# Down rows of the experts' MLP loaded as row pairs, 64 partitions and 8 KB each, with the inner columns transposed at a step of two

## The reference

```
DEPTH, SEQ, D_MODEL = 2, 256, 1024
N_EXPERTS, TOP_K_EXPERTS, D_FF_EXPERT = 8, 2, 2816

def swiglu(h, w_gate, w_up, w_down):
    a = jnp.einsum('bsd,df->bsf', h, w_gate)
    u = jnp.einsum('bsd,df->bsf', h, w_up)
    return jnp.einsum('bsf,fd->bsd', jax.nn.silu(a) * u, w_down)

def moe_swiglu(h, w_router, w_gate, w_up, w_down):
    logits = jnp.einsum('bsd,de->bse', h.astype(F32), w_router.astype(F32))
    top_val, top_idx = lax.top_k(logits, TOP_K_EXPERTS)
    top_w = jax.nn.softmax(top_val, axis=-1)
    combine = jnp.sum(jax.nn.one_hot(top_idx, N_EXPERTS, dtype=F32) * top_w[..., None], axis=-2)
    out = jnp.zeros_like(h)
    for e in range(N_EXPERTS):
        out = out + combine[..., e:e + 1].astype(h.dtype) * swiglu(h, w_gate[e], w_up[e], w_down[e])
    return out
```

## Time and profile before

| What | Value |
|---|---|
| runs | 1917.53, 1920.16, 1922.07 us; median 1920.16 us |
| profiled execution | 1927.55 us, of which the span of the records is 1925.7 us |
| mean granted TensorE clock | 0.98 |
| busy, share of the span | PE 95%, PEld 77%, DVE 74%, ACT 58%, POOL 20% |
| moved | 506.45 MB, mean 263 GB/s over the span |
| expert layer's loads | 176 transfers of 512 KB for each of gate, up and down |

### The profile page before, as it was taken

One profiled execution on the slowest core, in us unless ns is written; L12 is line 12 of the kernel. 1 busy time (PEld: TensorE's weight loads), 2 busy tenths in 40 slices (PEclk: granted clock), 3 DMA queues, 4 the chain that ended last, 5 costly groups with the idle time before them and its releaser, 6 DMA issues.

```text
span 1925.7 us, 26024 instructions
## 1 busy us (share of the span) xinstructions
PE 1832.6 (95%) x8799; PEld 1490.6 (77%) x8799; DVE 1420.1 (74%) x1631; ACT 1123.4 (58%) x1296; POOL 391.4 (20%) x315
## 2 busy tenths in 40 slices
PE   7899999989999997899989879999999999999997
PEld 5677886867888685788878667888888888888885
DVE  6647874465877477554566848898888888888897
ACT  5645443564444356344344727777777777777775
POOL 3722212453220365200036500000000000000000
PEclk9999999989999999899999989999999999999999
DMA  8338985416988441365645058999999999999994
GB/s 269 110 110 328 363 331 179 131 67 253 336 336 294 138 146 44 114 211 179 205 143 170 23 207 326 387 377 384 377 385 378 382 377 386 380 375 382 378 387 171
DMA packets 237934, 506.45 MB, mean 263 GB/s; under 512 B 23304, under 2 KB 74720, under 8 KB 231712
## 3 DMA queue, kind: packets, MB, share of 16 engines
q1 hardware_dynamic: 225664, 492.91, 70.5%
q0 software_dynamic: 3008, 10.32, 2.0%
q10 hardware_dynamic: 9184, 2.23, 0.5%
HBM read 497.49 MB, written 7.91 MB: 262 GB/s over the span
## 4 chain that ended last, share of the span: by engine, by line
PE 77%; DVE 8%; issue 7%; ACT 3%; POOL 2%; DMA 2%; SPq 0%; POOLq 0%; DVEq 0%; ACTq 0%
PE bank L2352 23%; PE bank L2354 23%; PE bank L2353 23%; PE bank L2471 2%; ACT slab L2043 1%; DVE slab L1291 1%; PE bank L2791 1%; POOL w_lo L827 1%; ACT w_hi L1893 1%; PE bank L2562 1%; PE bank L2540 1%; PE bank L2522 1%; DVE w_lo L978 1%; DMA slab<-in_w_mlp_out 1%; DMA slab<-in_w_router 1%
## 5 line engine op out<-in xcount | busy, mean ns | idle before, releaser
L978 DVE TENSOR_TENSOR w_lo<-slab,w_hi 128x2048 fp32r<-128x2048 f32 x369 | 847.3, 2305 | 219.0 <-ACT w_hi L1893 218.1
L1893 ACT ACTIVATE w_hi<-slab 128x2048 fp32r<-128x2048 f32 (+2 forms) x421 | 797.1, 1899 | 330.5 <-PE bank L2354 229.7
L2352 PE MATMUL bank<-w_hi,hT_hi 128*128 128x512 f32 (+3 forms) x1664 | 649.6, 390 | 15.0 <-DVE hT_lo L1027 4.3
L2354 PE MATMUL bank<-w_hi,hT_lo 128*128 128x512 f32 (+3 forms) x1664 | 638.1, 383 | 0.0
L2353 PE MATMUL bank<-w_lo,hT_hi 128*128 128x512 f32 (+3 forms) x1664 | 637.9, 383 | 0.0
L2352 PEld LDWEIGHTS bank<-w_hi,hT_hi 128*128 128x128 f32 x1664 | 316.4, 190 | 78.7 <-DVE w_lo L978 8.8
L2354 PEld LDWEIGHTS bank<-w_hi,hT_lo 128*128 128x128 f32 x1664 | 315.4, 190 | 59.7
L2353 PEld LDWEIGHTS bank<-w_lo,hT_hi 128*128 128x128 f32 x1664 | 316.4, 190 | 55.3
L827 POOL TENSOR_TENSOR w_lo<-slab,w_hi 128x512 fp32r<-128x512 f32 (+2 forms) x208 | 262.0, 1293 | 384.8 <-ACT w_hi L1893 365.2
L2352 PE MATMUL bank<-w_hi,hid_hi 128*128 128x512 f32 x680 | 266.6, 392 | 4.2 <-DVE hid_lo L1560 3.5
L2354 PE MATMUL bank<-w_hi,hid_lo 128*128 128x512 f32 x680 | 265.6, 391 | 0.0
(11 more groups left out here) (252 smaller groups left out, 1243.2 us busy)
## 6 DMA issues: line engine op xcount, KB each, us to landing
slab<-in_w_exp_gate SPq DMA_DIRECT2D x176, 512.0 KB, 7.0
slab<-in_w_exp_up SPq DMA_DIRECT2D x176, 512.0 KB, 7.2
slab<-in_w_exp_down SPq DMA_DIRECT2D x176, 512.0 KB, 6.9
slab<-in_w_ada SPq DMA_DIRECT2D x48, 1024.0 KB, 5.0
slab<-in_w_mlp_in SPq DMA_DIRECT2D x64, 512.0 KB, 6.2
slab<-in_w_mlp_out SPq DMA_DIRECT2D x64, 512.0 KB, 6.2
slab<-in_w_in SPq DMA_DIRECT2D x56, 512.0 KB, 5.0
slab<-in_w_out SPq DMA_DIRECT2D x32, 512.0 KB, 4.5
```

Of the source, the lines that this page charges most:

```text
L978: dve.tensor_tensor(w_lo[:, q, 0:n], raw(s)[:, 0:n], w_hi[:, q, 0:n].bitcast(F32), ALU.subtract).then_inc(lo_dve, 1)
L1893: act.activation(w_hi[:, q, 0:n], raw(s)[:, 0:n], ACT.Copy).then_inc(hi_done, 1)
L2352: pe.matmul(dst, a_hi, b_hi, start=start, stop=False)
L2354: return pe.matmul(dst, a_lo, b_hi, start=False, stop=stop_)
```

## The change

Three edits. The first is in how SP builds its transfers: `tile` makes the list of a tile's parts before it waits for the slot, where it made them one by one after the wait. The second is the layout of the experts' down tiles. `row_pairs` sees the weights as "(r p i) n -> p (a r) (i n)" with i = 2: partition p of row block r holds the rows 256 r + 2p and 256 r + 2p + 1, which lie side by side in memory, 8 KB. A tile is the same 256 rows and the same 1 MiB of memory as before, in another arrangement, and its two parts are partitions 64 to 127 and then 0 to 63, each 64 partitions x 8 KB. The third follows from the second: block i of a tile now holds every second down row, so `turn_hidden` with `pairs` set, which only the experts use, takes every second inner column of a block of 256 for each transpose. The other layers keep `rows` and plain columns.

```
--- before.py
+++ after.py
@@ -620,9 +620,10 @@
 
                 prev = ring.before_raw()
                 t, s, _, _ = ring.next()
+                moves = list(parts(raw(s)))
                 if prev is not None:
                     lo_wait(prev)
-                for dst, src in parts(raw(s)):
+                for dst, src in moves:
                     sp.dma_start(dst, src).then_inc(w_loaded[s], 16)
 
             def block_of(w, c, n, k0, nk):
@@ -654,6 +655,14 @@
                         d = r.rearrange("p (i n) -> p i n", i=2)
                         for i in (1, 0):
                             yield d[:, i:i + 1, :], w[:, bass.ds(r0 + 2 * b + i, 1), :]
+                    tile(parts)
+
+            def row_pairs(w, r0, n):
+
+                for b in range(n):
+                    def parts(r, b=b):
+                        for o in (P // 2, 0):
+                            yield r[o:o + P // 2, :].unsqueeze(1), w[o:o + P // 2, bass.ds(r0 + b, 1), :]
                     tile(parts)
 
             def ada_piece(l, k, n):
@@ -740,7 +749,8 @@
 
                         def weights(e):
                             return [A[n][0, bass.ds(e, 1)].rearrange("a (k p) n -> p (a k) n", p=P)
-                                    for n in ("w_exp_gate_2", "w_exp_up_2", "w_exp_down_2")]
+                                    for n in ("w_exp_gate_2", "w_exp_up_2")] + [
+                                        A["w_exp_down_2"][0, bass.ds(e, 1)].rearrange("a (r p i) n -> p (a r) (i n)", p=P, i=2)]
 
                         def body(i, p, n, first, last):
                             wg, wu, wd = weights(2 * i + p)
@@ -753,14 +763,14 @@
                                     sp.wait_ge(sc_done, 2 * (UNIT0[l] + UNITS[l]))
                                 cols(wg, wide_at(j + 1), F_WIDE)
                                 if narrow(j):
-                                    rows(wd, 0, 1)
+                                    row_pairs(wd, 0, 1)
                                 else:
-                                    rows(wd, 4 * j - 2, 2)
+                                    row_pairs(wd, 2 * j - 1, 2)
 
                             def final(j):
                                 if not last:
                                     gated(*weights(2 * i + p + 1)[:2], 0)
-                                rows(wd, 4 * j - 2, 2)
+                                row_pairs(wd, 2 * j - 1, 2)
 
                             step(0, first and n0 == 0)
                             step(1)
@@ -2464,12 +2474,16 @@
                         if c and not t:
                             between()
 
-            def turn_hidden(at, ntt, n, src, width_, dst):
+            def turn_hidden(at, ntt, n, src, width_, dst, pairs=False):
                 for t in range(ntt):
                     pe.wait_ge(sq_done, at + t + 1)
                     for f in range(n):
-                        ins = pe.transpose(dst[t][:, f * P:(f + 1) * P],
-                                           scr(src + t * width_ + f * P, P), ident)
+                        if pairs:
+                            two = scr(src + f // 2 * 2 * P, 2 * P).rearrange("p (q i) -> p i q", i=2)
+                            ins = pe.transpose(dst[t][:, f * P:(f + 1) * P], two[:, f % 2, :], ident)
+                        else:
+                            ins = pe.transpose(dst[t][:, f * P:(f + 1) * P],
+                                               scr(src + t * width_ + f * P, P), ident)
                     ins.then_inc(ht_done, 1)
 
             pe.wait_ge(c_in, 16)
@@ -2898,7 +2912,7 @@
                                 rows_of([bank[0]], listed_left, COL, 4, 4, False, True, 1)
 
                         def turn(j):
-                            turn_hidden(ub + n * MS + j, 1, 2 if narrow(j) else 4, X_MACT2, F_WIDE, [bank[0]])
+                            turn_hidden(ub + n * MS + j, 1, 2 if narrow(j) else 4, X_MACT2, F_WIDE, [bank[0]], True)
 
                         rows_up(0)
                         if not first:
```

4 lines of the change are left out of this document (2 added, 2 removed).

## The result

| What | Before | After |
|---|---|---|
| median of 4 runs | 1920.95 us (1917.53 to 1922.07) | 2261.24 us (2257.32 to 2266.44) |
| ratio to before, 95% interval | | 1.1768 (1.1743 to 1.1794) |
| span of the profiled execution | 1925.7 us | 2255.5 us |
| mean granted TensorE clock | 0.98 | 0.96 |

What follows compares the result with a forecast made beforehand. TensorE was taken to bound the kernel, with loads taking over after the change: +192.2 us for doubled down parts, -6.7 us at the tail, other terms nothing, +185.5 us in all, 2106 us; range 1917 to 2140 us.

Steps and rivals of the forecast that it cites:

- What bounds the kernel: Expert layer: TensorE sets the pace, 93.7 us per expert, waiting for no load; loads come early enough.
- 31 us of slack: Expert layer's loads: at 399 GB/s they would fit into 686 of 717.5 us, so slower loads use this up first.
- Two other signs: Expert layer, if right: down parts' time to landing grows above that of the others', and SP's waits stay.
- Half the partitions: Down tile loads: 64-partition parts cost between nothing and twice the time each; +192.2 us taken; chance of slowed loads 0.68.
- the slow end: Down parts: half the partitions find half of the shared ways into the SBUF, so each part takes twice the time.
- The tail: End of the stage: without a backlog, last landing to last VectorE split shrinks from 11.3 to 4.6 us, 6.7 us less.
- Longer rows: Down loads: 8 KB rows save at most 6 us of DMA time, worth nothing on the path.
- Stepped transposes: Experts' 176 transpose weight loads: 0 to 24.5 us, taken as nothing; rival that they cost, 1925 to 1945 us, chance 0.09.
- the lower bound: Stepped transposes cost nothing: a 188 ns contiguous load beside matmuls every 227 ns is free, and TensorE's idle time hides it.
- Addresses: SP's issue: making the list before the wait shifts register operations by tens of ns and moves nothing.
- The clock: Expert layer: TensorE at 79% busy might lose a little granted clock, hidden by idle time; no term.
- own range: Slowed loads: 1994 us if parts partly overlap, each down part costing half more; 2146 at 382 GB/s, put at 2140.

Runs made afterwards that it cites:

- the third kernel: The changed kernel with parts of 64 partitions and 8 KB rows, but odd partitions, then even ones, in place of upper and lower halves; 1924.35 us, ratio 1.0012 to before.

## Why the prediction was right or wrong

**What bounds the kernel: right.** TensorE set the pace with 31 us of slack in the loads. Every kernel whose loads kept their rate stayed within 0.2% of before, and every one whose loads slowed moved its whole stage; the waits of TensorE for the split and of ScalarE for a DMA came. Two other signs did not: the down parts land no later than the up parts, 15.8 and 15.9 us, and SP waits for slots 34% of the time, where it was 58%.

**Half the partitions: right in kind.** The choice of the slow end, made without a row that could price it, is shown by the third kernel against the change. The 31 us of slack can't be seen by itself; it is kept in the sums above as the trace of before gave it.

**The size of this term: wrong.** This is the step that failed. The forecast had "At twice the time each, the queue's work from 1178.5 us is 273.86 + 89.1 = 363.0 MB-equivalents, over 0.399 = 909.7 us". It took 1047.0 us, 137 us more, and two assumptions of that sentence are the reason. It let the engines be busy at a share of 1.04 all the time; at the share of 0.96, 1047.0 us hold the work of 1047.0 x 0.96 / 1.04 = 966 us, so 81 us are idle engines. And it left full parts at their old rate: the remaining 966 - 910 = 56 us are packets that took longer than the doubling of the down parts explains. The shares have two digits, so each of the two numbers is good to about 10 us. The packets bear it out: those of the gate and up parts took 17% longer, a term that the forecast put at nothing without a reason, and a byte of a down part took 1.77 times as long and not twice. So the doubling itself was put too high; by the kernel with all tiles in halves it is 2.2 us per tile and not 2.63, and the loss by mixture is then more like 85 x 0.43 + 137 = 174 us, an estimate, about half of the change's cost.

**The tail: nearly right.** The forecast took 6.7 us back, since without a backlog the 11.3 us from about 1896 us to the end of the last split should shrink to 4.6. The last split on VectorE is now this row, beside the earlier trace rows:

```profile
2234.98 2.29 DVE L988 TENSOR_TENSOR w_lo<-slab,w_hi 128x2048 fp32r<-128x2048 f32 x1 [0.54 <-ACT w_hi L1903]
```

It ends at 2237.27 us, 5.6 us after the last landing at 2231.6 us; before it was 9.9 us after the one at 1897.4 us. So the backlog did go, and 5.6 us stand against the 4.6 of the forecast. What it left out is that in ScalarE's order the copy of the transposed inner columns stands ahead of the last split, and waits for TensorE's transposes, before and now:

```profile
1902.61 0.60 ACT L2180 ACTIVATE hT_hi<-bank 128x512 fp32r<-128x512 f32 x1 [1.41 <-PE bank L2471]
2232.54 0.60 ACT L2190 ACTIVATE hT_hi<-bank 128x512 fp32r<-128x512 f32 x1 [1.42 <-PE bank L2483]
```

The loads are what came late. From 2225.5 us to the end of the span are 30.0 us, before from 1896 us 29.7; the forecast had 29.7 - 6.7 = 23.0. Of these 7.0 us, 6.1 are the one late engine's loads, from 2225.5 to 2231.6 us. With 137.3 us and these 7.0 us the span's 144.3 us over the forecast are accounted for: 2255.5 - 2111.2.

**Longer rows: right.** 8 KB rows in alternate partitions against 4 KB rows: 1924.35 and 1924.17 us.

**Stepped transposes: right in the sum, wrong in the row.** The forecast said they keep 139 ns; they take 202. The Trainium skill, "SBUF — State Buffer", section "Door 1: The DMA port swizzle (why `[64,N]` ≈ `[32,N]`)", has 16-byte lines where two hits keep full rate; the time of the load does not bear that out. The cost at the end is nothing, for the reason given for the lower bound.

**Addresses: right.** The list alone changes nothing (1.0006, 0.9992 to 1.002).

**The clock: nearly right.** The forecast had no term for it. The granted clock of the stage was 0.94 and not 1.00, a mean of stretches at the upper of its two levels, 2.4 GHz, and some at the lower, 1.2 GHz. Products of both kinds stand near the end of the stage (start us, us):

```profile
2219.10 0.79 PE L2362 MATMUL bank<-w_hi,hT_hi 128*128 128x512 f32 x1 [2.38 <-DVE w_lo L988]
...
2219.69 0.63 PE L2363 MATMUL bank<-w_lo,hT_hi 128*128 128x512 f32 x1
...
2220.12 0.63 PE L2364 MATMUL bank<-w_hi,hT_lo 128*128 128x512 f32 x1
...
2222.21 0.40 PE L2363 MATMUL bank<-w_lo,hT_hi 128*128 128x512 f32 x1
...
2222.44 0.39 PE L2364 MATMUL bank<-w_hi,hT_lo 128*128 128x512 f32 x1
```

After a wait of 2.38 us the products follow each other by 0.43 us, and 3 us later by 0.23 us. In a stage where TensorE has over 200 us of idle time this can hide, and in the kernel with all tiles in halves a clock of 0.92 goes with fully busy DMA engines, so it isn't what sets the pace there. For the change itself no run takes the clock apart from the loads.

**The chances and the range.** Slower had 0.76, and that was right. The forecast's own range, 1994 to 2140 us, reached 112 us down, to halves that overlap, and 34 us up, and the time was 121 us above its upper end. Both ends supposed engines that are always busy. A sum of bytes over a best rate allows for no idle engine; for the upper end one would have needed a row in which engines stand still with work outstanding, or in which slow parts slow their neighbours. The trace of before had neither, so the end should have stood much higher.

## What to carry to other kernels

Keep both halves of the partitions in every large transfer; if a transfer must cover 64 partitions, take every second one, which cost nothing here. If a few loads are made slow in the ways they use, do not price them alone: in this kernel 39 half tiles among 264 cost 5.1 us each where a stream of nearly nothing but half tiles cost 2.2. A tile is there when its last sixteenth is there, so look at the spread of the landings too. Once a queue has lost its cushion, read the share of the DMA engines together with the rate, in slices short enough to show holes: a page that shows 9 tenths everywhere hid 8% of idle time.

## What the runs showed of the hardware

- Parts in one half of the partitions, one after the other and alternating between halves, move 227 GB/s at a DMA share of 1.04 (31 of 33 tiles in halves). With full parts alone, or with down parts over every second partition, it is 380 GB/s at the pace TensorE asks for; 8 KB packets take 326 ns on average over every second partition and 591 ns in halves.
- Half parts mixed with full ones leave DMA engines idle with work outstanding: shares of 0.95 to 1.00, slices of 0.4 us at 1 tenth, and one issue on SP lasting up to 8.3 us. The 2 KB packets of the full parts take 103.5 ns on average, 88.5 without halves.
- One engine in sixteen is then last by far: 30 of a tile's 32 landing reports come within 4.0 us, the last 9.1 us later; without halves 2.4 and 0.7 us.
- A weight load of 128 columns that lie 8 bytes apart takes 202 ns; contiguous, 139 ns. The matmuls of such transposes took 280 ns, 271 with contiguous columns. Neither showed in the time.
